# First modulation, projection and recurrence of the first block as one stage on Trainium2

## The reference

```python
mod = silu(c) @ w_ada + b_ada            # six vectors of 1024; the first two are shift and scale
u = normalize(x) * (1 + scale) + shift
x_lru, y_lru, q, k, v = split(u @ w_in)  # five times 512 columns
xc = causal_conv(x_lru, conv_w) + conv_b # four taps along the tokens
r, i = sigmoid(xc @ w_gate_a + b_a), sigmoid(xc @ w_gate_x + b_x)   # block diagonal
log_a = -8 * r * softplus(-lambda)
h = scan(exp(log_a), sqrt(-expm1(2 * log_a)) * i * xc)
lru_out = h * gelu(y_lru)
attn_out = attention(q, k, v, bias by distance)   # 8 heads of 64
```

## Time and profile before

| | us |
|---|---|
| median of three executions | 3357.75 |
| lowest, highest | 3355.56, 3359.49 |
| profiled execution, its own time | 3357.08 |
| span of the profiled execution | 3355.3 |
| TensorE matmul busy in the span | 3087.2 (92%) |
| VectorE busy | 2436.8 (73%) |
| ScalarE busy | 1681.3 (50%) |
| GpSimd busy | 134.3 (4%) |
| mean granted TensorE clock | 0.933 |

### The profile page before, as it was taken

How to read it: one execution, slowest core, us unless ns; L and a number is a source line. 1 busy time by engine, 2 the same in 40 slices (tenths; PEclk the granted TensorE clock), 3 DMA queues, 4 the chain that set the end, 5 groups by cost and what they waited for, 6 DMA issues and landing times. The chain is left out here.

```text
span 3355.3 us, 58574 instructions
## 1 busy us (share of the span) xinstructions
PE 3087.2 (92%) x23849; PEld 2749.8 (82%) x23849; DVE 2436.8 (73%) x3652; ACT 1681.3 (50%) x2445; POOL 134.3 (4%) x152
## 2 busy tenths in 40 slices
PE   7779999889998899999988899999899999988899
PEld 6567777779887789898976899899689898978798
DVE  6568999878776478787578587785678787674655
ACT  4437777654552354545553444544554545442444
POOL 0010000000102000000000000000000000011000
PEclk8779999989998799999997899999899999998899
DMA  9346999757510267586430377674067686300442
GB/s 380 146 171 277 369 367 371 319 208 305 203 70 3 77 250 305 231 307 263 161 140 1 144 293 284 252 306 168 29 246 305 233 306 261 121 2 7 186 186 82
DMA packets 77661, 699.20 MB, mean 208 GB/s; under 512 B 8448, under 2 KB 12544, under 8 KB 55552
## 3 DMA queue, kind: packets, MB, share of 16 engines
q1 hardware_dynamic: 31072, 526.18, 40.0%
q10 hardware_dynamic: 42912, 157.31, 12.4%
q0 software_dynamic: 3456, 12.58, 1.0%
HBM read 691.84 MB, written 4.19 MB: 207 GB/s over the span
## 5 line engine op out<-in xcount | busy, mean ns | idle before, releaser
L1076 PE MATMUL banks<-u_split,w_split 128*128 128x512 f32 x2816 | 1017.4, 404 | 23.7 <-DVE u_split L1321 21.0
L1145 ACT ACTIVATE w_split<-ring 128x1024 fp32r<-128x1024 f32 x513 | 541.0, 1058 | 667.8 <-PE banks L1077 404.7
L1252 DVE TENSOR_TENSOR w_split<-ring,w_split 128x1024 fp32r<-128x1024 f32 x513 | 625.6, 1223 | 283.2 <-ACT w_split L1145 279.8
L1077 PE MATMUL banks<-u_split,w_split 128*128 128x256 f32 x2816 | 798.2, 283 | 0.0
L1076 PEld LDWEIGHTS banks<-u_split,w_split 128*128 128x128 f32 x2816 | 538.2, 191 | 160.8 <-issue 17.4
L1077 PEld LDWEIGHTS banks<-u_split,w_split 128*128 128x128 f32 x2816 | 540.9, 192 | 0.0
L1069 PE MATMUL banks<-h_split,w_split 128*128 128x256 f32 x1408 | 398.4, 283 | 0.0
L1068 PE MATMUL banks<-h_split,w_split 128*128 128x256 f32 x1408 | 398.3, 283 | 0.0
L1070 PE MATMUL banks<-h_split,w_split 128*128 128x256 f32 x1408 | 398.2, 283 | 0.0
L520 PE MATMUL banks<-bufs_split,ring_split 128*128 128x256 f32 x1376 | 397.5, 289 | 0.0
L584 DVE CUSTOM_DVE_ANT_0 bufs<-bufs 128x1024 f32<-128x1024 f32 x300 | 357.0, 1225 | 12.0 <-DVE w_split L1252 12.0
(11 more groups left out here) (489 smaller groups left out, 4928.9 us busy)
## 6 DMA issues: line engine op xcount, KB each, us to landing
ring<-stream SPq DMA_DIRECT2D x155, 3072.0 KB, 10.9
bufs<-ada ACTq DMA_DIRECT2D x296, 512.0 KB, 10.3
bufs<-ada POOLq DMA_DIRECT2D x23, 512.0 KB, 6.7
bufs<-ada SPq DMA_DIRECT2D x3, 2048.0 KB, 15.9
ring<-stream SPq DMA_DIRECT2D x2, 2688.0 KB, 9.7
bufs<-c_rows SPq DMA_DIRECT2D x10, 512.0 KB, 4.5
ring<-stream SPq DMA_DIRECT2D x1, 2704.0 KB, 13.5
ring<-stream SPq DMA_DIRECT2D x1, 2176.0 KB, 8.8
```

The lines of the kernel that those rows point to most:

```text
L1076: pe.matmul(bank.rearrange("p (a t) -> p a t", a=2), w_high, u_split[:, k, :, :], start=(k == 0), stop=False, skip_group_check=True)
L1077: return pe.matmul(bank[:, 0:SEQ], w_low, u_split[:, k, 0, :], start=False, stop=(k == KC - 1), skip_group_check=True)
L1145: nc.scalar.activation(w_split[:, slot, 0, :], piece(j, b), ACT.Copy).then_inc(high.sem, 1)
L1252: e = nc.vector.tensor_tensor(w_split[:, slot, 1, :], piece(j, b), w_split[:, slot, 0, :].bitcast(F32), ALU.subtract)
```

## The change

Three stages become one, `first_stage`. The columns of w_in for x, y and q (12 blocks) are stored by chunk: eight pieces ("w_xyq", k) of 1,536 columns, four to a unit; k keeps its four blocks of 1,024. w_ada comes in 16 slices of 0.5 MB, two per chunk (shift and scale), in eight slots, four chunks ahead, mixed on SyncE's queue with the pieces. For each chunk VectorE sums its two slices, adds the start values, scales the chunk and splits; TensorE then adds that chunk's 36 products to six open banks of sums (12 blocks of 256 columns), cleared beforehand. High parts of pieces take turns in two slots. The mean and the sum of squares are made with a matrix of ones so that sums stand on all partitions; GpSimd's additions and the spreading matmuls go. The distance rows are made four ahead of the mean and four behind the sum of squares. After x, y and q come two k blocks, the gates, two k blocks, and v; the convolution (its copy and first tap now on ScalarE), gates, recurrence and the five slices stand beside them. The bias rows are read back, and the five slices loaded, once x, y and q are done. The logarithm series for the decay rates moves to the start. Three ring slots are counted as freed at the stage's end only.

```diff
+FIRST_BLOCKS = (2 * D_LRU + D_ATTN) // P
...
-    blocks("w_in", D, 2 * D_LRU + 2 * D_ATTN)
+    plan += [(("w_xyq", k), FIRST_BLOCKS * P) for k in range(KC)]
+    blocks("w_k", D, D_ATTN)
...
-        self.slots = [*b(7), core.bufs[:, 1, D:2 * D], core.bufs[:, 5, D:2 * D], core.state[:].rearrange("p a n -> p (a n)"),
+        self.slots = [*(core.ring[:, 0, q * D:(q + 1) * D] for q in range(5)),
...
-def first_ada_stage(core, x_in, cent, squares):
...
-def first_projection_stage(core, rows, shift, raw, xc, y_act, qk, v_tok, later):
...
+def first_stage(core, x_in, qk, v_tok, lru_out, bias, later):
...
+    B, AHEAD = FIRST_BLOCKS, 4
+    width = B * P
...
+    ada_slots = [flat(i, at) for i in (8, 4, 5, 2) for at in (0, D)]
+    u = (core.split_buf(6), core.split_buf(7))
+    high_slots = [split(1, 0, width), split(9, 0, width)]
+    k_slots = [split(3), core.w_state[:], core.ring_split[1][:, 4 * D:5 * D], core.ring_split[1][:, 5 * D:6 * D]]
+    v_slots = [core.ring_split[1][:, q * 2 * D:(q + 1) * 2 * D] for q in range(2)]
...
+            def load_ada(c):
+                if c >= AHEAD:
+                    sync.wait_ge(step.sem, step.at(2 * (c - AHEAD) + 2))
+                for part in range(2):
+                    half = 2 * part + c // 4
+                    sync.dma_start(ada_slots[2 * (c % AHEAD) + part], core.ada[half, :, (c % 4) * D:(c % 4 + 1) * D])\
+                        .then_inc(ada_loaded[c % AHEAD].sem, ada_loaded[c % AHEAD].count(16))
+
+            def load_piece(c):
+                unit, at, n, _ = core.place[("w_xyq", c)]
+                done = core.loaded[unit] if c % 4 == 3 else piece_loaded[c % 4]
+                if c >= 4 and c % 4 < 3:
+                    wait_piece(sync, c - 4)
+                sync.dma_start(core.ring[:, unit, at:at + n], core.stream[core.rows[unit], :, at:at + n]).then_inc(done.sem, done.count(16))
+
+            sync.dma_start(table[0:REL_BUCKETS, :], core.rel_bias).then_inc(rows_loaded.sem, rows_loaded.count(16))
+            at, n = const_plan()[0]["buckets"]
+            sync.dma_start(buckets[0:REL_BUCKETS + 1, :], core.consts_dram[0:REL_BUCKETS + 1, at:at + n])\
+                .then_inc(rows_loaded.sem, rows_loaded.count(16))
+            sync.dma_start(core.x[:], x_in.rearrange("(c p) t -> p c t", p=P)).then_inc(x_loaded.sem, x_loaded.count(16))
+            sync.dma_start(core.cols[:, 0:early_cols], core.cols_dram[:, 0:early_cols]).then_inc(cols_loaded.sem, cols_loaded.count(16))
+            sync.dma_start(c_row, core.c_rows[0:1, :].to_broadcast([P, D])).then_inc(c_loaded.sem, c_loaded.count(16))
+            load_ada(0)
+            load_ada(1)
+            load_piece(0)
+            sync.dma_start(core.consts[:], core.consts_dram[:, 0:const_plan()[0]["band"][0]]).then_inc(consts_loaded.sem, consts_loaded.count(16))
+            load_ada(2)
+            load_piece(1)
+            for c in range(3, KC):
+                load_ada(c)
+                load_piece(c - 1)
+            load_piece(KC - 1)
+            core.loaded_units = 2
+            sync.wait_ge(distances.sem, distances.at(HEADS_A))
+            core.load_ahead(sync, None, 3)
+            for q in range(2):
+                sync.wait_ge(copied.sem, copied.at(4 * q + 4))
+                sync.dma_start(core.scratch[:, 4 * q:4 * q + 4, :], rows[q].rearrange("p (h j) -> p h j", h=4))\
+                    .then_inc(rows_stored.sem, rows_stored.count(16))
+            sync.wait_ge(rows_stored.sem, rows_stored.at(32))
+            core.load_ahead(sync, None, 4)
+            sync.dma_start(core.cols[:, early_cols:], core.cols_dram[:, early_cols:]).then_inc(cols_loaded.sem, cols_loaded.count(16))
+            sync.wait_ge(step.sem, step.at(2 * KC))
+            sync.wait_ge(projected.sem, projected.at(B // 2))
+            for t in range(2):
+                for h in range(HEADS_A):
+                    src = bass.AP(core.scratch.tensor, h * 2 * SEQ + (SEQ - 1) - t * P, [[HEADS_A * 2 * SEQ - 1, P], [1, SEQ]])
+                    sync.dma_start(bias[:, h, t, :], src).then_inc(read.sem, read.count(16))
+            core.load_ahead(sync, ("gate_x", 0))
+            sync.wait_ge(read.sem, read.at(16 * 16))
+            sync.wait_ge(cols_loaded.sem, cols_loaded.at(32))
 
         @block.gpsimd
         def _(pool):
-            pool.wait_ge(rows_stored.sem, rows_stored.made)
+            pool.wait_ge(projected.sem, projected.at(B // 2))
             later.load(pool, LATER_SUMS["recurrence"])
...
+            def chunk_products(c):
+                pe.wait_ge(low.sem, low.at(c + 1))
+                pe.wait_ge(u_low.sem, u_low.at(c + 1))
+                w = (high_slots[c % 2], piece(c, low=True))
+                for b in range(B):
+                    last = three_products(pe, pair(b // 2)[:, b % 2, :], [part[:, b * P:(b + 1) * P] for part in w],
+                                          [part[:, c, :] for part in u], False, c == KC - 1)
+                    if c == KC - 1 and b % 2:
+                        last.then_inc(projected.sem, projected.count(1))
+                if c < KC - 1:
+                    last.then_inc(chunk_used.sem, chunk_used.count(1))
...
+            distance_rows(0, 4)
+            pe.wait_ge(constants_ready.sem, constants_ready.at(2))
+            pe.wait_ge(x_loaded.sem, x_loaded.at(16))
+            sums(MEAN_BANK, core.x, None, x_summed)
+            sums(ROOT_BANK, squares, squared, square_sums)
+            distance_rows(4, HEADS_A)
+            pe.wait_ge(constants_ready.sem, constants_ready.at(3))
+            pe.wait_ge(centered.sem, centered.at(KC // 2))
+            pe.wait_ge(scaled.sem, scaled.at(1))
+            for bank in range(4):
+                clear(bank)
+            pe.wait_ge(copied.sem, copied.at(6))
+            for bank in range(4, B // 2):
+                clear(bank)
+            for c in range(KC):
+                chunk_products(c)
...
+            k_block(0)
+            k_block(1)
+            pe.wait_ge(convolved.sem, convolved.at(4))
+            gate(0, "gate_a")
+            pe.wait_ge(evacuated.sem, evacuated.at(2))
+            gate(1, "gate_x")
+            k_block(2)
+            k_block(3)
...
+                    v_block(p, t)
+            pe.wait_ge(step.sem, step.at(2 * KC + len(LATER_SUMS["recurrence"])))
+            pe.wait_ge(projected.sem, projected.at(B // 2 + 8))
+            for unit in range(3):
+                pe.nop().then_inc(core.freed.sem, core.freed.count(1))
...
+            def piece_high(c):
+                wait_piece(act, c)
+                if c >= 2:
+                    act.wait_ge(chunk_used.sem, chunk_used.at(c - 1))
+                act.activation(high_slots[c % 2], piece(c), ACT.Copy).then_inc(high.sem, high.count(1))
...
+            copy_rows(0, 4)
+            center_on_scalar(core, act, cent, squares, centered, squared)
+            piece_high(0)
+            act.wait_ge(scaled.sem, scaled.at(1))
+            act.activation(core.rstd[:], core.rstd[:], ACT.Sqrt).then_inc(rooted.sem, rooted.count(1))
+            act.wait_ge(consts_loaded.sem, consts_loaded.at(16))
+            act.activation(core.zeros[:].rearrange("p (a t) -> p a t", t=P), core.const("zeros").unsqueeze(1).to_broadcast([P, 4, P]), ACT.Copy)\
+                .then_inc(constants_ready.sem, constants_ready.count(1))
+            copy_rows(4, HEADS_A)
             for c in range(KC):
-                apply_shift(core, act, u[0], rows, shift, c, u_high)
-                if c in (0, 2, 4):
-                    weight_high(core, act, c // 2, keys[c // 2], slots, projected)
-            for b in range(3, 16):
-                weight_high(core, act, b, keys[b], slots, projected)
-                if b % 2 == 0 and b >= 8:
-                    evacuate(b // 2 - 2)
-            for p in range(2):
-                unit = core.place[("w_v", p)][0]
-                act.wait_ge(core.loaded[unit % SLOTS].sem, 16 * (unit // SLOTS + 1))
-                if p == 0:
-                    act.wait_ge(convolved.sem, convolved.at(2))
-                act.activation(v_slots[p], v_piece(p), ACT.Copy).then_inc(v_high.sem, v_high.count(1))
-                evacuate(6 + p)
+                apply_shift(core, act, u[0], cent, sh, c, u_high)
+                if c + 1 < KC:
+                    piece_high(c + 1)
+            for b in range(2):
+                late_high(("w_k", b), k_slots[b], high)
...
+            for b in range(2, 4):
+                late_high(("w_k", b), k_slots[b], high)
+            late_high(("w_v", 0), v_slots[0], v_high)
+            act.wait_ge(projected.sem, projected.at(B // 2 + 2))
+            act.activation(qk[:, 4:6, :], pair(6), ACT.Copy)
+            for g, (dst, column) in enumerate(((gate_r, "b_gate_a"), (gate_i, "b_gate_x"))):
+                act.wait_ge(gate_sums.sem, gate_sums.at(g + 1))
+                for c in range(4):
```

(51 more changed lines are left out.)

363 lines of the change are left out of this document (161 added, 202 removed).

## The result

Twenty runs of each kernel on one chip gave a median of 3363.38 us (3358.52 to 3370.61) after the change, against 3355.94 us (3347.55 to 3360.95) before it: a ratio of 1.0024, with a 95% interval of 1.0018 to 1.0031. The forecast was 3365 us, 7.25 above the median first shown; the measured difference is 7.4 us. The change makes the kernel a little slower, by 7 us in one set and 13 to 15 in the other.

The account below looks back on a forecast made before the run. TensorE was taken to lie uncovered some 43 us before the projection and 22 behind it. Attention starting 8.5 us later, less 1.0 within attention, gave +7.5 us: forecast 3365 us, range 3350 to 3376.

Parts of the forecast that it names:

- Start: Stage start to the first x, y, q products: 31 to 34 us, taken as 32, against 43.4 before.
- The chain: Chunk loop: each start of chunks 1 to 6 waits for copy, subtraction and small split; TensorE idle 4.0 us each.
- The clock: Chunk loop: each pause lowers TensorE's clock, about 4.9 us low per chunk, so 36 matmuls take 6.5 us.
- rival 1: Chunk loop: clock stays high through the pauses, chunk 4.3 us, sum 15.4 lower; -8 us, 3350; chance 0.14.
- Sum to the end of x, y, q: Start plus chunk loop: 32.0 + 7 x 6.5 + 6 x 4.0 + 4.4 = 105.9 us.
- The rest of the stage: After x, y, q: k, v, gates and joints 27.7 us, then 1.5 + 0.5; attention starts at 135.6, 8.5 later.
- Attention: First attention stage: first scores halve at the high clock, which then falls; 1.0 us off.
- The bounds, 0 and 5.5: First attention stage: limits in us on its saving; 5.5 is half of some 11 us worked at low clock.
- Sum: Whole kernel: +8.5 at attention's start and -1.0 in attention give +7.5 us, forecast 3365 us.
- Rival 3: Stage tail: late bias reads or modulation slices hold the recurrence, 3 to 6 us; +12, 3370; chance 0.12.
- Rival 2: Chunk loop: clock never rises, chunk 7.7 us, 8.4 more; +16, 3374; chance 0.12.
- Rival 4: First attention stage keeps the high clock: 5.5 instead of 1.0 us off; +3, 3361; chance 0.14.

Follow-up runs that it names:

- e1: Changed kernel with chunk c's small split moved ahead of the next piece's low part on VectorE; 3334.60 us, ratio 0.9945 to the kernel before.
- e4: Changed kernel, order kept, with a third slot for high parts and unit 3 loaded later; 3336.72 us, ratio 0.9952 to the kernel before.
- e2: Changed kernel reordered: VectorE scales chunk c+1 and makes its piece's low part behind chunk c's split, ScalarE shifts before copying; 3327.56 us, ratio 0.9916 to before.
- after: The changed kernel in its first profiled execution, span 3358.8 us; median of its twenty runs 3363.38 us, ratio 1.0024 to the kernel before.
- a0: The changed kernel again, unaltered, on another chip (the second set); 3367.62 us against 3352.4 for the kernel before, ratio 1.0040.
- e3: Changed kernel with 14 matmuls of zeros on TensorE behind each of chunks 0 to 5; 3352.84 us, ratio 0.9997 to the kernel before.
- e5: e2 with matmuls of zeros around attention's start (8 behind v, 5 behind first scores, 8 before first transposes); 3322.26 us, ratio 0.9907 to the kernel before.
- e7: e5 with the four modulation slices for the sums behind attention issued by SP instead of POOL; 3318.64 us, ratio 0.9890 to the kernel before.

## Why the prediction was right, and where its terms were off

- **Start.** Forecast 31 to 34 us, taken 32; measured 32.04. The last wait was another: ScalarE's copies of the distance rows were done at 26.27 us, and VectorE held up chunk 0: behind the low part of piece 0 and the three additions stood the reciprocal of 256 columns. It took 1.75 us:

```profile
25.52 1.75 DVE L1660 RECIPROCAL rstd<-rstd 128x256 f32<-128x256 f32 x1
27.31 0.48 DVE L1633 SCALAR_TENSOR_TENSOR bufs<-bufs,mod,rstd 128x256 f32<-128x256 f32 x1
```

  The prediction named it without a price; that the start came out to 0.04 us is partly luck.
- **The chain.** Forecast six idle times of 4.0 us; measured 3.91 to 3.92. It is the order and the slot count together: undoing either (e1, e4) shortens the idle time to 2.2 or to 1.1 and 2.6 in turn, undoing the order at every step (e2) to 0.5.
- **The clock.** Forecast a fall in each pause and 6.5 us a chunk; measured a mean of 6.5 over the first seven bursts in after and 6.3 in a0. The fall came with every pause, but only five of the twelve falls in after and a0 lay inside it; seven came 0.6 to 1.3 us after TensorE had started again. So the mean came out right over bursts of two kinds (6.0 and 6.7 to 6.8 us) and a slow first one (7.27), which the forecast didn't tell apart. e3 prices the level: x, y, q end 12.3 us earlier, where rival 1 had put 15.4 on a clock that stays high. Rival 1 itself is refuted for this kernel. Shorter pauses are no safe way out: the clock fell at one pause of 2.17 us in e1 and at both of 2.57 us in e4, and stayed up at two others of 2.17 us.
- **Sum to the end of x, y, q.** Forecast 105.9, measured 105.3; a0 had 103.8, its first burst 6.33 us long in place of 7.27.
- **The rest of the stage.** Forecast 27.7 us of TensorE and 2.0 behind it; measured 26.6 (105.3 to 131.9) and 1.9. The prediction's 11.5 + 11.5 + 3.7 = 26.7 was right; the 1.0 for joints was not, there is no idle time between the blocks. SP's last issues bound the border, as forecast, with VectorE's end 0.5 us ahead of theirs (131.51 + 1.23 = 132.74 against 133.27):

```profile
131.51 1.23 DVE L1699 TENSOR_TENSOR bufs<-bufs 128x1024 f32<-128x1024 f32 x1
...
131.99 1.28 SPq L458 DMA_DIRECT2D ring<-stream  x3
...
133.82 2.08 PE L1728 MATMUL banks<-bufs 64*128 64x256 f32 x8 [1.91 <-PEq L1359]
```

  A table switch took 1.28 us, and the next ACTIVATE started 0.02 us behind it:

```profile
112.81 1.28 ACT L1591 ACT_TABLE_LOAD   x1
114.11 1.57 ACT L1591 ACTIVATE spare<-banks,cols_sb 128x256 f32<-128x256 f32 x4
115.55 1.58 ACT L1591 ACTIVATE bufs<-banks,cols_sb 128x256 f32<-128x256 f32 x4
```

  The dearer price of the Trainium skill (ScalarE: Activation LUTs, "What ACT_TABLE_LOAD costs", 2.66 us in all) doesn't show here: the four ACTIVATEs behind the switch are no longer than the next four.
- **Attention.** Forecast 1.0 us shorter. In the profiled execution of after it was not: the first scores took 2.08 us in place of the half of 2.09, since the clock had fallen at 133.8, at the end of the border's 1.91 us. In a0, the same kernel with the same idle time, it fell only at 135.2:

```profile
132.14 1.14 PE L1728 MATMUL banks<-bufs 64*128 64x256 f32 x8 [1.91 <-PEq L1359]
```

  The scores were halved, and from attention's start to the next stage's products a0 took 46.4 us in place of 47.3, 0.9 less; e1, e3 and e4, whose border is the same, read 46.4 us too, and e2 47.2. So the term of 1.0 us was sized right for the executions in which the clock holds over the border, and was missing in the one profiled first. The bounds, 0 and 5.5, held both ends: e5 got 5.3 us by keeping TensorE busy through the border.
- **Sum.** In the profiled execution of after, attention's start was forecast 8.5 us later and was 6.7; its length -1.0 and was 0: +7.5 against +6.7 at the next stage's products, two errors that went against each other. In a0 the start was 5.0 later and the length -0.9: +4.1. The median moved by 7.4, but part of this agreement is luck: what stands behind the rewritten stage varied by more than the whole difference, and the second set read 13 to 15 us. The runs show the direction and the mechanism; they don't show the size to within some us.
- **Rival 3** (late slices or bias reads hold the recurrence) didn't happen: VectorE's end is 0.5 us before SP's. **Rival 2** (never high) neither. **Rival 4** (attention keeps the high level) neither: where the clock did hold over the border (a0, e1, e3, e4), it fell 1.9 to 3.1 us after the first scores had begun.

## What to carry to other kernels

When a loop over chunks is fed by several engines, write down, for each engine, what stands ahead of the one small instruction that the consumer waits for: here 0.4 us of work stood behind 3.2 us of the next chunk's, and moving one line was worth 27 us in the traces, about four times what the whole change had lost. Covering idle stretches of one engine gained nothing here, because the new order made a ring of waits out of work that used to be ready. After removing a wait look at the next border: of e5's 5.3 us, 2.3 went to transfers that had been in time until then, and most of the rest to the border before and to the clock behind. And compare places in the traces, not only whole times: here whole times moved by several us for reasons that lie outside the rewritten stage.

## What the runs showed of the hardware

- While TensorE multiplied zeros in the pauses its clock stayed at the high level: 1.00 from 36 to 93 us in e3, where the loop without them read 0.75.
- With each of twelve idle times of 3.9 us (after, a0) the clock went to the low level: five times during it, seven times 0.6 to 1.3 us after dense products had started again. It also fell with both idle times of 2.57 us in e4 and with one of the three of 2.17 us in e1.
- A border of 1.91 us left the clock high in a0 and low in after, the same kernel: 1.14 and 2.08 us for the same eight matmuls.
- In e7 the clock fell 1.8 us after dense work had ended, while one-column matmuls ran.
- A stage in whose program POOL had issued transfers ended only when they had landed (e5, e5b); with SP as the issuer it didn't wait (e7).
- VectorE's reciprocal of 128x256 took 1.75 us, where the scaling of as many columns took 0.48.
